# Fewer repeated matmuls of constants on TensorE at seven places of a four-layer trunk

## The reference

```python
for i in range(DEPTH):                       # 4
    kind, j = i % N_MIXERS, i // N_MIXERS
    hp = _modulate(_rmsnorm(xp, norm1[i]), mp[0], mp[1])
    hs = _modulate(_rmsnorm(xs, norm1[i]), ms[0], ms[1])
    ...                                      # attention / pooling / retention
    xp = xp + mp[2] * yp
    xs = xs + ms[2] * ys
    hp = _modulate(_rmsnorm(xp, norm2[i]), mp[3], mp[4])
    hs = _modulate(_rmsnorm(xs, norm2[i]), ms[3], ms[4])
    xp = xp + mp[5] * _moe(hp, *moe_args)
    xs = xs + ms[5] * _moe(hs, *moe_args)

def _moe(h, ...):
    pg = softmax(t @ w_rg + b_rg); p_top, g_idx = top_k(pg, 1)
    le_sel = (t @ w_re + b_re) of the chosen group
    pe_top, e_idx = top_k(softmax(le_sel), 2)
    gates = one_hot(expert_id, 16) weighted by p_top * pe_top / sum(pe_top)
    act = silu(t @ w_gate) * (t @ w_up) * gates
    return act @ w_down
```

## Time and profile before

| what | value |
|---|---|
| median of 3 runs | 1555.09 us (1554.6 to 1555.68) |
| the profiled execution | 1555.1 us, of which the span from first to last instruction is 1553.3 us |
| mean granted TensorE clock | 0.978 |
| PE busy | 1450.3 us, 93% of the span |
| DVE, ACT, POOL busy | 765.2, 324.6, 85.0 us |
| HBM traffic | 436 MB, 281 GB/s over the span |

### The profile page before, as it was taken

The page is one execution under the profiler, slowest core; times in us unless marked ns, Lnnn a source line. Parts: engine busy times, 40 slices in busy tenths (PEclk is TensorE's granted clock), DMA queues, the critical chain, the costliest instruction groups (busy, mean ns, idle before and its releaser), DMA issues. The chain is left out here.

```text
span 1553.3 us, 18260 instructions
## 1 busy us (share of the span) xinstructions
PE 1450.3 (93%) x6691; PEld 763.8 (49%) x6691; DVE 765.2 (49%) x1849; ACT 324.6 (21%) x707; POOL 85.0 (5%) x97
## 2 busy tenths in 40 slices
PE   5998999999679999999999999999999998999975
PEld 3334536444246443556666666465444446464432
DVE  1234204653566544566666666036545464156534
ACT  1105304111223111511111111032112225131101
POOL 0000010000220001000000000010001010100001
PEclk9999999999889999999999999999999999999997
DMA  9989968899896998745555554546998730059995
GB/s 358 386 316 366 387 242 324 347 423 422 327 349 236 422 422 343 269 151 177 176 178 177 178 175 139 231 177 251 420 423 344 302 115 1 28 221 395 424 422 203
DMA packets 152278, 436.87 MB, mean 281 GB/s; under 512 B 6944, under 2 KB 63104, under 8 KB 123136
## 3 DMA queue, kind: packets, MB, share of 16 engines
q1 hardware_dynamic: 136816, 396.93, 67.0%
q10 hardware_dynamic: 11920, 26.24, 4.4%
q0 software_dynamic: 3456, 12.58, 2.3%
HBM read 414.20 MB, written 21.53 MB: 281 GB/s over the span
## 5 line engine op out<-in xcount | busy, mean ns | idle before, releaser
L1012 PE MATMUL bank<-gate_up_weights,hT_gathered 128*64 128x512 f32 (+1 forms) x1280 | 255.7, 599 | 17.5 <-SPq L542 16.4
L1012 PEld LDWEIGHTS bank<-gate_up_weights,hT_gathered 128*64 128x64 f32 (+1 forms) x1280 | 82.9, 133 | 182.6 <-issue 182.1
L845 PE MATMUL bank<-panel,hT 128*128 128x512 f32 x384 | 166.3, 592 | 0.9 <-ACT hT L1951 0.9
L1026 PE MATMUL bank<-down_weights,actT 128*64 128x512 f32 (+1 forms) x640 | 138.5, 603 | 2.5 <-ACT actT L2165 1.7
L1441 DVE SCALAR_TENSOR_TENSOR ada_sums<-panel,cond_columns,ada_sums 128x384 f32<-128x384 f32 x224 | 121.2, 611 | 0.0
L845 PEld LDWEIGHTS bank<-panel,hT 128*128 128x128 f32 x384 | 72.9, 190 | 89.0 <-issue 87.5
L656 PE MATMUL bank<-panel,hT 128*128 128x512 f32 x240 | 105.0, 595 | 0.9 <-ACT hT L1951 0.9
L997 PE MATMUL bank<-h_hi,P 128*128 128x512 f32 x216 | 92.2, 427 | 0.0
L656 PE MATMUL bank<-panel,oT 128*128 128x512 f32 x192 | 84.3, 595 | 1.3 <-ACT oT L2069 1.3
L997 PE MATMUL bank<-h_lo,P 128*128 128x512 f32 x216 | 85.2, 394 | 0.0
L2152 ACT ACTIVATE silu<-bank 128x256 f32<-128x256 f32 x36 | 13.8, 384 | 309.9 <-PE bank L1012 309.9
(11 more groups left out here) (332 smaller groups left out, 1986.7 us busy)
## 6 DMA issues: line engine op xcount, KB each, us to landing
gate_up_weights<-in_gate_up_halves SPq DMA_DIRECT2D x148, 1024.0 KB, 13.8
down_weights<-in_down_rows SPq DMA_DIRECT2D x74, 1024.0 KB, 13.9
panel<-in_w_ada SPq DMA_DIRECT2D x27, 2048.0 KB
panel<-in_w_ada SPq DMA_DIRECT2D x16, 1536.0 KB
ada_panel_third<-in_w_ada SPq DMA_DIRECT2D x9, 2048.0 KB
y_by_slot<-y_rows ACTq DMA_DIRECT2D x32, 512.0 KB, 8.1
panel<-in_ret_w_in SPq DMA_DIRECT2D x16, 1024.0 KB
panel<-in_attn_w_qkv SPq DMA_DIRECT2D x5, 2048.0 KB
```

The lines of the kernel that those rows point to most:

```text
L845: last = PE.matmul(ps[t][:], hT[:, k, t * 128:(t + 1) * 128], panel[f % 2][:, k, :], start=k == 0, stop=k == KD - 1)
L1012: last = PE.matmul(ps[2][width * s:width * s + width, :], hg[:, j, k, width * s:width * s + width], gu_ring[w][:, 2 * k // KD, :, k % (KD ...
L1026: last = PE.matmul(ps[6 + half][width * s:width * s + width, :], actT[:, c, width * s:width * s + width], dn_ring[w][:, c, half * 512:half ...
```

## The change

Every count that `pe_keep_busy` is given is lowered; one call goes. No other instruction is added, removed or moved. Over the four layers the calls of `PE.matmul` at L583 go from 109 to 62.

```diff
@@ pe_route
         pe_turn(pe, n, 1)
         parts(0)
         if l > 1:
-            pe_keep_busy(pe, 10)
+            pe_keep_busy(pe, 6)
         pe_turn(pe, n, 2)
...
         tokens(1)
         tokens(2)
         if l:
-            pe_keep_busy(pe, 5)
+            pe_keep_busy(pe, 2)
         pe.wait_ge(sem("assigned"), l + 1)
...
         PE.matmul(ps[6][:, 176:192], ones[:], asg[:, 2, :], start=False, stop=True).then_inc(sem("ranks"), 1)
-        pe_keep_busy(pe, 5)
+        pe_keep_busy(pe, 2)
@@ the loop over layers
                 if l > 1:
-                    pe_keep_busy(pe, 12)
+                    pe_keep_busy(pe, 11)
                 pe_turn(pe, 2 * l, 0)
                 if l > 1:
-                    pe_keep_busy(pe, 9)
+                    pe_keep_busy(pe, 7)
...
             pe_row_gather(pe, l, 0, 1)
-            pe_keep_busy(pe, 3)
             pe_row_T(pe, l, 0)
```

## The result

| | before | after |
|---|---|---|
| median of the runs | 1555.38 us (4 runs) | 1546.24 us (4 runs, 1544.55 to 1546.75) |
| profiled execution | 1555.1 us, span 1553.3 | 1546.53 us, span 1544.7 |
| mean granted TensorE clock | 0.978 | 0.979 |

The ratio is 0.9937, 95% interval 0.9922 to 0.9952: 9.8 us faster (7.5 to 12.1) where 11.5 was forecast, and 1546.24 lies inside the range of 1540.7 to 1547.8. The same kernel run again beside the experiments gave 1543.02 us (5 runs), ratio 0.9916 (0.9900 to 0.9933), 13 us faster. In the mean its nine runs took 1544.6 us, and the 73 runs of the kernel before that stand beside the experiments 1555.8: 11.2 us. (The places in the code whose count changes are six, not the seven of the title.)

A forecast was written before the change was run, and what follows sets the result against it. PE (TensorE), busy 93% of the span, was taken as the bound. Gains of 1.05, 1.55, 5.1 and 3.8 us in layers 0 to 3 summed to 11.5: 1555.1 - 11.5 = 1543.6 us, range 1540.7 to 1547.8.

The forecast's parts named there:

- Between the first gather and its transposes: All layers, three calls to none: gate/up starts 1.05 us earlier per layer, with VectorE's copy of the second half late next.
- Behind the ranks: All layers, five calls to two: gain 0, since the gather's second half waits for VectorE's last `h_lo` anyway.
- Before the ranks: Layers 1 to 3, five calls to two: ranks then follow the assignment, 0.5 us gained in layer 1, more in layer 2.
- Before the turn of tile 2: Layers 2 and 3, ten calls to six: the turn starts when VectorE's half is scaled, 1.55 us earlier.
- the branch with fast tokens: Layer 2, ranks: if the tokens run fast the assignment decides, gain 3.75 us; with slow tokens 2.75.
- At the start of layers 2 and 3: Twelve calls to eleven, nine to seven: projections start earlier by 1.3 us in layer 2 and 0.7 in layer 3.
- I leave the number of falls elsewhere as it was: Outside the stretch from tokens to gather, clock falls were assumed unchanged in number; no new fall was counted, size 0.
- More falls: Rival: each routing has one more clock fall, on tokens or gather, 1.66 to 2.6 us each: 1552.1 us, chance 0.13.
- a sign of being wrong: New stretches of granted clock at 0.50 between tokens and the first gate/up would show the prediction wrong; no size given.
- Hidden by the transfers: Rival: DMA paces the rows, so routing gains return as waits and only the starts count: 1553.1 us, chance 0.04.
- The clock stays low into the first row: Rival: a fall at the gather lasts through row 0's gate/up, 11 us a layer: 1587 us, chance 0.03.
- Constants off the path: Rival: the cuts at the starts of layers 2 and 3 are hidden, losing 2.0 us: 1545.6 us; no chance given.

The follow-up runs named there:

- Experiment 5: Kernel before with only the calls behind the rank matmuls cut from five to two, all layers: 1556.41 us, ratio 1.0009.
- experiment 3: Kernel before with only the calls before the wait for the assignment cut from five to two, layers 1 to 3: 1552.71 us, ratio 0.9977.
- experiment 1: Kernel before with only the three calls between the first gather and its transposes removed, all layers: 1551.27 us, ratio 0.9975.
- experiment 4: Kernel before with only the starts of layers 2 and 3 cut, twelve calls to eleven and nine to seven: 1552.83 us, ratio 0.9988.
- experiment 11: Kernel before with twelve calls added in the idle waits of layer 3's attention: 1553.95 us, ratio 0.9994.
- `attn_only`: The same run as experiment 11: kernel before with twelve calls added in layer 3's attention, 1553.95 us, ratio 0.9994.
- the two filled ones: Changed kernel with twelve calls added in the idle waits of layer 3's attention, run twice: 1540.12 us and 1538.62 us.
- Experiment 2: Kernel before with only the calls before the turn of tile 2 cut from ten to six, layers 2 and 3: 1550.98 us, ratio 0.9972.
- 6: Changed kernel with all its remaining 62 calls removed: 1555.39 us, ratio 1.0001 to the kernel before.
- 7: Changed kernel without its 26 routing calls, the 36 at the starts of layers 2 and 3 kept: 1550.55 us, ratio 0.9966.
- 9 to 11: Twelve calls added in layer 3's attention: twice in the changed kernel, 1540.12 and 1538.62 us, once in the kernel before, 1553.95 us.

## Why the prediction was right, and where not

**Between the first gather and its transposes: right.** 1.0 us per layer (forecast 1.05), by the mechanism named, with VectorE's copy next in line. The small rest is that the second half of the gather came 0.1 us later behind the ranks than before (4.79 against 4.69 us in layer 1).

**Behind the ranks: right.** Experiment 5 has nothing, and the wait moved to the second half of the gather.

**Before the ranks: right in its mechanism, 0.25 us too small.** The queue's load was taken for the matmul's start (experiment 3).

**Before the turn of tile 2: right,** 1.73 for 1.55. In layer 2 the fall over the tokens, which the forecast had left where it was, was in no profile of the changed kernel, and that stage measured 1.73 + 2.39 = 4.12, beyond the "gain 3.75" of the branch with fast tokens. But 1.66 of it is luck: experiments 1, 4 and 11 show the same 1.66 at this place and do not touch it. The forecast took a fall of one execution for a property of the code.

**At the start of layers 2 and 3: the term was mis-sized.** The prediction said "Three calls less: 1.3 us, to 632.5, still behind `hT`". In the profile after the stage gained 0.12 (rows of layer 1 included), in two others 1.6, where kernels with unchanged starts gained 0.4 to 1.0; the runs of experiment 4 leave 1.9 us for both layers together, not told from nothing. The step that failed is that `hT` was taken to be ready when it was before. VectorE copies its half of `hT` behind the scaling of tile 1, and both hang on gathered rows that land at times of their own: counted from the first constant matmul, this half stood at 7.3 us in the kernel before (624.11 to 631.37) and at 10.0 in the one after (619.40 to 629.36).

**"I leave the number of falls elsewhere as it was": not so in the profiles, and open for the change.** The changed kernel's two profiles lose 1.6 to 1.7 us in retention and 2.7 to 3.0 in the attention of layer 3, 4.4 to 4.6 together, against the one profile of before. These falls came behind idle waits in the mixers, where in these layers there never were any constants, and the waits had not become longer (2.29 and 2.30 us before L875). Whether the change brings them is not shown. In retention there was a fall in both profiles of the changed kernel and with four of the five single edits, none with the fifth (experiment 1), none in the kernel before, in `attn_only` and in one of the two filled ones. The attention spent 10.2 us at half clock in both profiles of the changed kernel, and 3.4, 10.2, 0, 6.8, 3.4 and 0 us in the six profiles of the kernel before and of experiments 1 to 5. Experiment 2 has its longest wait unfilled, and no fall behind it:

```profile
1282.98 0.98 PE L742 MATMUL bank<-const_base,prob 128*128 128x128 f32 x7 [2.88 <-DVE prob L1363]
```

Nor did the whole become slower in clock: the mean granted clock was 0.978 over the 73 runs of the kernel before and 0.979 over the nine of the changed one. What is shown is the other direction: where calls were taken away altogether, falls came (6 and 7), and the three profiles with the attention's waits filled have none there (9 to 11).

The Trainium skill, "TensorE: Matmul & The Clock Gate", section "Part 1: The HAM clock gate (the "warmup" mystery)", says of a kernel's start that how many matmuls pass before the clock rises differs from run to run of one kernel. The traces agree, for a place in the middle of the program: the same retention code with the same 2.3 us wait had a fall at 665.0 in one and none in another.

**Why the sum came out near.** Against the profile of before, gains that the forecast did not have stand against the falls: the 1.66 over layer 2's tokens, 1.37 over layer 0's rows and the mixer of layer 1 (0.51 and 1.18 in the other two), and 1.05 in the last rows (1.46, 1.99). The last is chance too, since profiles with untouched last rows gained up to 1.65 there. The 1.37 was tested by no experiment. So the 8.6 us of one pair of profiles are near for a sum whose parts partly cancel. The mean of the runs, 11.2 us for 11.5, is the better test. Of it the routing's terms are shown one by one: from the table, without the 1.66, they come to 3.8 us between gather and gate/up, 2.3 before the ranks and 3.5 before the turn of tile 2, 9.6 us where 9.5 were forecast. The other 2.0, for the starts, are not shown.

**The rivals.** *More falls* had each routing one fall richer. From the tokens to gate/up the profile of before had two (layers 0 and 2), those of this routing one, two, one and one. So it did not come, though a stretch in layer 3 (1371.6) is what the prediction had named as a sign of being wrong. *Hidden by the transfers* is out: experiment 1 keeps its gain. (The prediction's "1.01" for the DMA share is in no row that it names; the earlier trace rows has 0.99.) *The clock stays low into the first row* did not come: after each fall over a gather the clock was back before or at the first gate/up. *Constants off the path*, for the starts, is not excluded: three of the six starts in the table are within 0.4 us of nothing, and the other three gained 0.5 us or more beyond what unchanged starts did.

## What to carry to other kernels

A filler matmul costs its own time only where it outlasts the wait it covers: compare its end with the end of what the next real instruction needs, and cut it back to just that. Then look for idle waits of 2 us and more that have no filler at all, since that is where the clock fell, in some executions, in code that nobody touched; filling those was worth 4 us in the changed kernel beside the 10 of trimming, and in the kernel before no difference that can be told. Since such falls come and go, do not read them from one profile: compare the mean clock of many runs and profiles of code that is the same at the place. And do not conclude from "less filler was faster" that none would be best: of 109 calls 47 cost 10 to 13 us, and the other 62 earned as much.

## What the runs showed of the hardware

- A fall of the clock does not follow from the length of a wait alone: 2.28 to 2.30 us of idle before the same instruction ended at full clock in two profiles shown here and at half clock in a third; 2.88 us before L742 ended at full clock in experiment 2.
- The attention of layer 3 took 1.4 us longer with 3.4 us of it at half clock than with none, and 4.1 to 4.4 us longer with 10.2 us.
- TensorE's half clock over a gather makes a 512-column matmul 0.63 us instead of 0.40, and eight transposes of a turn 1.97 us instead of 1.04.
- A rank matmul that TensorE had to wait for started 0.01 us behind its weight load; behind other work in the queue it started 0.22 us behind.
- Two executions of the same code differed by up to 1.5 us at one layer's start, by VectorE's waits for rows that an indirect DMA brings.
